# Index scores of two stages: from one head at a time to two heads whose matmuls are issued in turn

## The reference, cut to what matters

```python
B_IDX_HEADS, B_IDX_DIM = 4, 64
# iq: 4 heads of 64 channels; ik: one head of 64 channels, shared by the four
logit = jnp.einsum('bqhd,bsd->bqhs', iq_c, ik)
idx_score = jnp.einsum('bqhs,bqh->bqs', jax.nn.relu(logit), iw_c)
idx_score = jnp.where(key_pos[None, :] <= t_pos[:, None], idx_score, -jnp.inf)
_, sel = lax.top_k(idx_score, n_keep)
```

## Time and profile before

| | us |
|---|---|
| three runs | 3522.08, 3524.36, 3529.35 |
| median | 3524.36 |
| profiled execution | 3526.53 |
| its span in the trace | 3524.8 |
| index block of h0: first score matmul to next product | 2226.14 to 2238.91 |
| index block of h1 | 2888.97 to 2897.62 |

### The profile page before, as it was taken

The page is one execution under the profiler, slowest core; times in us unless marked ns, Lnnn a source line. Parts: engine busy times, 40 slices in busy tenths (PEclk is TensorE's granted clock), DMA queues, the critical chain, the costliest instruction groups (busy, mean ns, idle before and its releaser), DMA issues.

```text
span 3524.8 us, 38806 instructions
## 1 busy us (share of the span) xinstructions
PE 3299.1 (94%) x16388; PEld 2704.5 (77%) x16388; DVE 1748.7 (50%) x2494; ACT 1155.1 (33%) x1505; POOL 154.0 (4%) x228
## 2 busy tenths in 40 slices
PE   4999999999999999999799998889999998899998
PEld 4887895769888988887598888656777886567687
DVE  5455552325555533355543335685644458765434
ACT  3222335243222322234632223333452233335322
POOL 0000001010000000001100000000000010000000
PEclk7999999999999999999899998989999999899898
DMA  4555440403555223323122321422212232222121
GB/s 175 174 180 184 156 144 0 156 13 128 191 178 178 90 97 100 99 76 107 52 85 99 101 89 49 117 60 66 66 60 84 84 90 76 74 60 72 60 96 48
DMA packets 286550, 353.71 MB, mean 100 GB/s; under 512 B 9458, under 2 KB 263210, under 8 KB 286378
## 3 DMA queue, kind: packets, MB, share of 16 engines
q1 hardware_dynamic: 286378, 351.23, 30.4%
HBM read 336.00 MB, written 2.10 MB: 96 GB/s over the span
## 4 chain that ended last, share of the span: by engine, by line
PE 81%; DVE 11%; ACT 5%; issue 1%; DMA 1%; POOL 1%; SPq 0%; DVEq 0%; ACTq 0%; POOLq 0%
PE psum L566 55%; PE psum L686 6%; PE psum L1049 3%; PE psum L645 2%; PE psum L755 2%; PE psum L587 2%; PE psum L918 2%; PE psum L956 2%; DVE w_low L1601 1%; PE psum L934 1%; DVE psum L1729 1%; PE psum L744 1%; PE psum L532 1%; PE psum L767 1%; DVE h_low L1741 1%
## 5 line engine op out<-in xcount | busy, mean ns | idle before, releaser
L566 PE MATMUL psum<-h_high,w_high 128*128 128x512 f32 (+1 forms) x2496 | 986.5, 395 | 34.7 <-DVE y_plain L2003 11.6
L566 PE MATMUL psum<-h_high,w_low 128*128 128x512 f32 (+1 forms) x2496 | 979.4, 392 | 0.0
L566 PE MATMUL psum<-h_low,w_high 128*128 128x512 f32 (+1 forms) x2496 | 979.2, 392 | 0.0
L1601 DVE TENSOR_TENSOR w_low<-raw,w_high 128x2048 fp32r<-128x2048 f32 (+2 forms) x246 | 540.3, 2206 | 354.6 <-ACT w_high L1117 354.4
L1117 ACT CAST w_high<-raw 128x2048 fp32r<-128x2048 f32 (+3 forms) x254 | 464.5, 1842 | 530.6 <-DMA raw<-in_ffn_w_gu 226.8
L566 PEld LDWEIGHTS psum<-h_high,w_high 128*128 128x128 f32 (+1 forms) x2496 | 473.3, 190 | 143.4 <-issue 16.7
L566 PEld LDWEIGHTS psum<-h_high,w_low 128*128 128x128 f32 (+1 forms) x2496 | 472.5, 189 | 101.1
L566 PEld LDWEIGHTS psum<-h_low,w_high 128*128 128x128 f32 (+1 forms) x2496 | 473.4, 190 | 98.4 <-issue 0.5
L566 PE MATMUL psum<-y_high,w_high 128*128 128x512 f32 x608 | 242.2, 398 | 29.9 <-DVE y_low L1767 16.5
L1844 DVE TENSOR_TENSOR area<-area,psum 128x512 f32<-128x512 f32 x88 | 60.2, 684 | 376.1 <-PE psum L566 367.7
L566 PE MATMUL psum<-y_low,w_high 128*128 128x512 f32 x608 | 239.7, 394 | 0.0
(11 more groups left out here) (268 smaller groups left out, 4425.4 us busy)
## 6 DMA issues: line engine op xcount, KB each, us to landing
raw<-in_ffn_w_gu SPq DMA_DIRECT2D x88, 1024.0 KB, 5.2
raw<-in_mod_w SPq DMA_DIRECT2D x72, 1024.0 KB, 4.9
raw<-in_w_in SPq DMA_DIRECT2D x64, 1024.0 KB, 5.1
raw<-in_ffn_w_down SPq DMA_DIRECT2D x32, 1024.0 KB, 7.0
raw<-in_ffn_w_down SPq DMA_DIRECT2D x16, 768.0 KB, 4.8
raw<-in_sb_w_qkv SPq DMA_DIRECT2D x12, 1024.0 KB, 5.2
area<-area SPq DMA_DIRECT2D x92, 128.0 KB, 2.4
raw<-in_lru_w_in SPq DMA_DIRECT2D x10, 1024.0 KB, 5.2
```

The costliest lines, as they stand in the source:

```text
L566: mm = e.matmul(psum[0:width, base + m, :], wv[a][:, at_k, c0:c0 + width], X[b][:, k, :], start=(at_k == 0 and (a, b) == (0, 0)), stop=(at ...
L1601: e.tensor_tensor(w_low[raw_at[m]][:, :n], raw[raw_at[m]][:, :n], w_high[x % NW][:, :n].bitcast(F32), ALU.subtract).then_inc(*q.up(s_low, ...
```

## The change

The four passes over heads become two passes over pairs of heads. In a pass, the matmul of tile n is issued for the even head and then for the odd head, and only then tile n+1 comes. One semaphore step tells the end of a pair instead of a head. The even and the odd head still use their own 64 rows and their own three banks. The second pair waits for both relus of the first pair before its first matmul. The relus of both heads of a pair wait for the pair's step.

```diff
-                for h in range(4):
-                    g, r0 = h % 2, (h % 2) * HD
-                    if h < 2:
-                        for bank in range(3 * g, 3 * g + 3):
+                for pair in range(2):
+                    for bank in range(6):
+                        if pair == 0:
                             wait_free(bank)
-                    else:
-                        q.wait_ge(*at("relu", stage, h - 2))
...
+                    if pair:
+                        for h in range(2):
+                            q.wait_ge(*at("relu", stage, h))
                     for n in range(NT):
-                        o = 1536 * g + ROW_AT[n]
-                        m = e.matmul(flat[:, o:o + P * (n + 1)], L.iq[r0:r0 + HD, h // 2, n * P:(n + 1) * P], L.ik[r0:r0 + HD, 0, 0:P * (n + 1)],
-                                     start=True, stop=True)
-                    m.then_inc(*q.up(s_attend, "i_scores", stage, h))
+                        for x in range(2):
+                            r0, o = x * HD, 1536 * x + ROW_AT[n]
+                            m = e.matmul(flat[:, o:o + P * (n + 1)], L.iq[r0:r0 + HD, pair, n * P:(n + 1) * P], L.ik[r0:r0 + HD, 0, 0:P * (n + 1)],
+                                         start=True, stop=True)
+                    m.then_inc(*q.up(s_attend, "i_scores", stage, pair))
...
                 for h in range(4):
-                    q.wait_ge(*at("i_scores", stage, h))
+                    q.wait_ge(*at("i_scores", stage, h // 2))
                     q.wait_ge(*(at("index_added", stage, h - 2) if h > 1 else at("iw", stage)))
```

More of the change, by code:

```diff
@@ L845, in hybrid @@
                 free[5] = [("iw", stage)]
-                for h in range(4):
-                    g, r0 = h % 2, (h % 2) * HD
-                    if h < 2:
-                        for bank in range(3 * g, 3 * g + 3):
-                            wait_free(bank)
-                    else:
-                        q.wait_ge(*at("relu", stage, h - 2))
[L853 to L856, removed]
-                    for n in range(NT):
-                        o = 1536 * g + ROW_AT[n]
-                        m = e.matmul(flat[:, o:o + P * (n + 1)], L.iq[r0:r0 + HD, h // 2, n * P:(n + 1) * P], L.ik[r0:r0 + HD, 0, 0:P * (n + 1)],
-                                     start=True, stop=True)
-                    m.then_inc(*q.up(s_attend, "i_scores", stage, h))
+                for m in range(2):
+                    q.wait_ge(*at("roped", stage, "i_q", 0, m))
+                q.wait_ge(*at("roped", stage, "i_k", 0, 0))
+                q.wait_ge(*at("copied_half", stage, "ik"))
+                for pair in range(2):
+                    for bank in range(6):
+                        if pair == 0:
+                            wait_free(bank)
+                    if pair:
+                        for h in range(2):
+                            q.wait_ge(*at("relu", stage, h))
+                    for n in range(NT):
+                        for x in range(2):
[3 more added lines that the diff above has]
+                    m.then_inc(*q.up(s_attend, "i_scores", stage, pair))
                 for bank in range(6):
```

## The result

The changed kernel takes 3542.39 us (median of 13 runs, 3530.34 to 3545.16), the kernel before 3527.34 beside it (13 runs, 3520.40 to 3541.27). The ratio is 1.0034, 95% interval 1.0019 to 1.0049: slower by some 12 us by the ratio (the two medians are 15 apart), where +3.6 was forecast and 3535 was the upper end. The runs of the changed kernel fall into two clusters: four at 3530 to 3533 (mean granted clock 0.959 to 0.960), nine at 3540 to 3545 (0.955 to 0.957). The profiled execution is one of the four: 3530.34 us, span 3528.6. So its trace can show the mechanism, but not the whole loss.

The account below looks back on a forecast made before the run. PE is busy 94% of the span, but in the index blocks PE and ACT take turns through heads and relus. Terms: +0.86 us in h0 and +2.7 in h1, total +3.6, median 3528.0; range 3521.5 to 3535.

Parts of the forecast that it names:

- The overlap and the order of waits: Index blocks: heads already overlap, so pairs gain PE 0.54 us; the second pair's wait for relu 1 costs 1.13 us.
- the gain ends under relu 0: First pair of h1: the 0.54 us that PE gains end under relu 0, where nothing waits for them.
- head 2's longer wait: Second pair in the index block: head 2 waits for relu 1 as well as relu 0, 1.13 us more.
- My lag of 0.2 us: Interleaved pairs: odd head starts 0.2 us behind the even head at full clock, 0.4 at half; bounds 0 and 0.74.
- two of my signs: In h1: the first pair takes 2.5 to 2.8 us, not 3.16; relu 0 starts 0.1 to 0.3 us later.
- the sum for h1 at full clock: h1's block goes from 8.65 to 10.17 us, +1.52; with lag 0 +1.12, with lag 0.74 +2.60.
- The clock term: PE pauses 2.4 us between pairs; h1 at +1.52, or +3.9 with half clock, middle +2.7; none behind the block.
- h0's sum: h0's block: first pair at half clock, clock back during the second; product at 2239.77 instead of 2238.91, +0.86.
- The rest: Outside the blocks: DVE's sums 1 to 3 us later fall into its 3.7 us wait; nothing else moves.
- Rival B: Longer pauses hold PE at half clock through both blocks: 2.2 us in h0, 6.3 in h1, together 8.5; chance 0.09.
- The spread: Whole kernel: three runs span 7.3 us, taken as 2 us to a side; about 0.2%, 7 us, can be told.

Follow-up runs that it names:

- x4: Idle matmuls in the index blocks' pauses and in the two later PE pauses, on the changed kernel (3526.49 us) and on the kernel before (3522.36 us).
- x1_after_again: The changed kernel unaltered, run again for a second profile: 3544.83 us, ratio 1.0038 to the kernel before.
- x3_after_late_busy: Changed kernel with idle matmuls only in the two later PE pauses, in front of attention heads 11 and 12: 3534.65 us, ratio 1.0014.
- x4_after_all_busy: Changed kernel with idle matmuls in the index blocks' three pauses and in the two later PE pauses: 3526.49 us, ratio 0.9997.
- late fill: Idle matmuls in PE's pauses in front of attention heads 11 and 12: kernel before 3523.06 us, changed kernel 3534.65 us.
- x3_before_shift: Kernel before with two idle matmuls per stage, some 20 us ahead of the pause in front of attention head 11: 3538.22 us, ratio 1.0023.

## Why the prediction was wrong

*The overlap and the order of waits: right.* Heads overlapped before, an interleaved pair costs about as much as a lone head, the gain ends under relu 0, and head 2's longer wait costs. My lag of 0.2 us was too long: 0.01 to 0.04 in the trace (2.43 against 2.42 us for a lone head, 4.64 against 4.60 at half clock), and so two of my signs failed: the pair took 2.43 us and not 2.5 to 2.8, and relu 0 started 0.02 us later and not 0.1 to 0.3. With lag 0 the sum for h1 at full clock was +1.12; x4's blocks, 9.9 against 8.7, have +1.2 in both stages. So this term is 2.4 us in the traces, and 4.1 between the medians.

*The clock term: the step that failed first, right in kind and several times too small.* "One of two lost it. [...] I take the middle, +2.7", "I take none and keep it for the range". In all three traces of the changed kernel without idle matmuls in the block, half clock covered both of h0's pairs, and h1's second pair or both pairs (11.4 and 13.2 us). h0's product then took 13.4 us in two of three traces of such blocks (x1_after_again and x3_after_late_busy; both have 13.2 in h1's block as well). Against the kernel before (11.1 + 11.0 in h0, 8.6 in h1) that is +5.6 and +4.6 us, 10 us together, where the forecast had 3.6 for wait and clock in both blocks (the first trace, with 11.0 for h0's product and 11.4 for h1's block, has 6). That the pauses are the cause is shown by x4_after_all_busy: with PE kept busy in them, on top of the late fills, the median fell by 8.2 us.

*The base of h0's sum: one execution was taken for the kernel.* The trace that I read has 12.8 us for h0's block and 12.6 for its product. Four traces of kernels with the block of before exist now, and the other three (the kernel again, with the late fill, with the shift) have 11.1 to 11.2 and 11.0. The timeline of the kernel before in its second trace:

```profile
2227.03 9.80 PE L859 MATMUL psum<-y_plain 64*128 64x128 f32 x32 [2.79 <-DMA y_plain<-y_plain]
...
2238.21 0.47 PE L566 MATMUL psum<-h_high,w_high 128*128 128x512 f32 x1 [1.37 <-ACT area L1408]
```

So my +0.86 for h0 was against a slow passage; against the common one it is +3.1 for the block.

*"The rest. [...] Nothing else moves": the second step that failed, a term put at nothing.* I let everything behind the block shift without changing length. The attention heads did start later by about the same, but a pause 220 us behind the block changes its price by up to 9 us per stage with a shift of some tenths. In the second trace of the changed kernel this is 9 of the 15 us by which it is longer than the first. What it adds to the difference of the medians is less sure: with the late pauses filled in both kernels, 11.6 of the 15.1 us stayed. No rival had it. Rival B named the half clock and stopped at the block; its price (8.5 us) was nearer to the result than the forecast.

*The spread.* Three runs within 7.3 us looked like noise. A good part of it is this: with the later pauses and the blocks filled, 11 or 12 runs lie within 5 to 9 us, where 13 runs of each plain kernel lay within 15 to 21.

Not settled: whether the changed kernel comes to the late pause at a bad moment more often than the kernel before does, and why. The plain traces have 1 long passage of 4 against 0 of 4, which is too few to tell, and I made no run that moves the changed kernel's pause back.

## What to carry to other kernels

Two row groups overlap already when their matmuls are issued one head after another, so ask what the trailing head hides before making both end together. Where PE alternates with one other engine, a step for a pair in place of a step per head makes PE's pauses longer, and here those pauses of 2.5 us cost more through the clock than by themselves. Matmuls that nobody reads, put into the block's pauses, were worth 8 us once the late pauses were filled too; in the kernel before, filling the block's pauses alone cost 7 us. So fill all the pauses that matter, or measure again. Don't take one trace's half-clock passages for the kernel's: look at two or three, and when a change of 1 us costs 10, look for a pause far behind it that now falls at another moment of the clock.

## What the runs showed of the hardware that wasn't expected

- Across row groups PE doesn't keep the order of the program. In the kernel before, head 1's first record, which the program has behind all of head 0's, began at 2889.71, and head 0's last three at 2890.03 to 2890.78; head 0 took no longer for it (2.44 us to its relu). Issued in turn, the 16 records of two groups take 2.43 us at full clock, and the 8 of one group 2.42.
- The same pauses (3.2 and 1.9 us) were followed by 3.4 us of half clock or by 10.2 to 20.5, by whether the first began 35.73 to 36.07 us behind the clock's last rise or outside of that, 22 times of 22. The limits come from these 22; the two passages of x3_before_shift were forecast.
- The kernel keeps step with the clock's changes up to h0's block. In all 16 traces PE's first instruction of h0's index block (line 843) starts 38.5 to 38.7 us behind the clock's last rise, while its time from the start of the program goes from 2220.8 to 2226.2 us. At h1's block it is one of two distances, 85.3 to 85.5 or 87.0 to 87.1. This would explain why a shift of a few tenths shows in a median and isn't lost in chance.
